# A delta rule layer whose heads draw their weight pieces from one chain, and new orders in two later layers

## The chip, the cores and the metric

The kernel runs on one core of a Trainium2 chip. The metric is the device time of one execution, in microseconds (us); lower is better.

## The reference, cut to what is computed

Two blocks of layers run over one sequence of 512 tokens, with a model width of 1024, all in fp32. The first block has a pooling mixer, a gated delta rule (the layer that most of the change is in), latent attention and again pooling. The second block has an even layer (Mamba, with a gated feed-forward in front and a causal depthwise convolution over its streams) and an odd layer (differential attention with rotary embedding). The delta rule has 8 heads; q and k have 128 rows, v and the gate z 256, and q, k and v first pass a causal convolution of 4 taps and a SiLU. Its core per head and chunk:

```python
def chunk_gated_delta_rule(q, k, v, g, beta):
    B, S, H, dk = q.shape
    dv = v.shape[-1]
    C = GDN_CHUNK
    N = S // C
    ...
    g = jnp.cumsum(g.reshape(B, N, C, H).transpose(0, 3, 1, 2), axis=-1)
    k_beta = k * beta[..., None]
    v_beta = v * beta[..., None]
    causal = jnp.tril(jnp.ones((C, C), dtype=bool))
    strict = jnp.tril(jnp.ones((C, C), dtype=bool), -1)
    diff = g[..., :, None] - g[..., None, :]
    decay = jnp.exp(jnp.where(causal, diff, -jnp.inf))
    L = jnp.where(strict, jnp.einsum('bhnid,bhnjd->bhnij', k_beta, k) * decay, 0.0)
    A = jnp.eye(C, dtype=L.dtype) + L
    rhs = jnp.concatenate([v_beta, k_beta * jnp.exp(g)[..., None]], axis=-1)
    sol = lax.linalg.triangular_solve(A, rhs, left_side=True, lower=True)
    u_ps = sol[..., :dv]
    w_cd = sol[..., dv:]
    attn = jnp.where(causal, jnp.einsum('bhnid,bhnjd->bhnij', q, k) * decay, 0.0)
    def step(state, xs):
        q_c, k_c, u_c, w_c, g_c, a_c = xs
        v_new = u_c - jnp.einsum('bhck,bhkv->bhcv', w_c, state)
        o = (jnp.einsum('bhck,bhkv->bhcv', q_c * jnp.exp(g_c)[..., None], state)
             + jnp.einsum('bhij,bhjv->bhiv', a_c, v_new))
        g_last = g_c[..., -1]
        k_dec = k_c * jnp.exp(g_last[..., None] - g_c)[..., None]
        state = state * jnp.exp(g_last)[..., None, None] + jnp.einsum('bhck,bhcv->bhkv', k_dec, v_new)
        return state, o
    ...
    _, o = lax.scan(step, state0, xs)
    return o.transpose(1, 0, 3, 2, 4).reshape(B, S, H, dv)
```

The result of a head is normalised, multiplied by its scale and by SiLU of z, and taken through the output weights.

## The kernel before, in words

A product of the large weights is done in pieces of 128 x 128 weights against 128 x 512 activations. Because the fp32 operands are split into a high and a low part, one piece is three matmuls (lines 334, 335 and 336), each one 128x512. Weights arrive by DMA as 128 x 1024 blocks, ScalarE (ACT) rounds the high part (`whi`, line 296) and GpSimd (POOL) makes the low part (`wlo`, line 311). VectorE (DVE) "takes" a finished product tile out of PSUM. Eight pieces make one tile of a projection. Tiles go round four PSUM banks, so the first piece of tile n waits until tile n-4 is taken.

The delta rule layer (about 325 to 870 us of the span) works head by head. Its own matmuls are small and wait on DVE and ACT. `work_tensor(pe, i, more)` (line 1933) is the order on TensorE (PE) for head i, and at each of 21 named sites it calls `more(site)`, which issues some pieces of the large products to fill the time. How many is a table, `PIECES` and `PIECES_BETWEEN`, at line 2318 and on. `pieces(i)` (line 2349) yields the 56 pieces that go with head i: V1 (the second half of the head's v), K of the next head, Q, V0, the gates z0 and z1 of 8 pieces each, and then four output tiles of 2 pieces each. When `work_tensor` of a head returns, a loop issues what is left of its pieces ("rest"). Head 0 also draws the first six pieces of head 1, so heads 1 to 4 have few left.

The sites in their order within a head: `kk` (k times k), `P2`, `P4`, `P8`, `PV8` (doubling steps of the triangular inverse), `X`, `X2`, `X2V`, `join`, `joined`, then for each chunk c of four `v new c`, `o c` and `kS c`. Ahead of `kk` there are three short pieces of work: the k tokens (`k_tokens`, line 1930, transposes of k), the sum over o of the head before (line 2044) and the row of the gate G (line 1963). The G row waits for "y gated 1" of the head before, since both use one bank. ACT starts from the k tokens: squares of k (line 2049), kdec (2055), the square of q (1923), ln (2141), ln o (2143), then exp (2073 and on), and at its end the N blocks (2083), for which P2 waits.

`work_vector(dve, i, fill, y_before)` (line 2163) is the order on DVE. Each `fill(site)` there makes as many takes as the table `TAKES` says; a take of q, k or v is followed by its four convolution taps (lines 1881 and 1884), spread behind later fills. For head 0 alone the set-up of the gates stands in front (`gate_vector`): six memsets (line 1810) of 128x512 or 128x256 zeros, then the rows of G in high and low parts (lines 1812 and 1814, "rows"), for which PE waits with the k tokens of head 0.

In the even layer `glu_vector` (line 1042) makes the convolution taps (line 1032) that follow the first product; `other_taps(dve, g, a)` (line 1197, work on line 1202) makes three taps of another stream. In the odd layer `rotary_tables` (line 2440) makes the cosine and sine tables of head pair 0; `cos`, `sin` (lines 3152 and 3159 to 3167) apply them, `square` (line 3124), `ln_k` (line 3130) and the exp of `lam` (line 3091) are ACT's, and the scores (line 3303) wait for kn (line 3172).

## Time and profile before

| | us |
|---|---|
| median of 3 runs | 2474.79 |
| lowest and highest | 2472.77, 2477.22 |
| the profiled execution, own time | 2474.79 |
| its span | 2473.0 |
| PE busy | 2435.5 (98%) |
| DVE busy | 1649.3 (67%) |
| POOL busy | 1191.4 (48%) |
| ACT busy | 1034.5 (42%) |
| PE clock over the span | 0.997 of full |

The profiled execution is the median run itself, so a change to its span can be set against the median directly; 1.8 us lie outside the span. Busy time of PE is modelled, with each matmul shown from its start to an end that overlaps the next. How long a matmul really holds the engine is the distance from its start to the next one's. DVE is busy in two thirds of the span, and in stretches where it is late, PE waits; an idle time of an engine other than PE costs nothing unless PE waits for it.

### The profile page before, as it was taken

The page shows a single profiled execution, that of the slowest core. Times are in us where ns is not written, and L with a number is a line of the kernel's source. Part 1 is how long each engine was busy: PE and PEld are TensorE (multiplying, and loading weights), DVE is VectorE, ACT ScalarE, POOL GpSimd, SP SyncE. Part 2 cuts the span into 40 slices and gives each one's busy share as a digit, 9 for nine tenths or more (in the row PEclk, how much of TensorE's full clock was granted, in tenths as well). Part 3 has the DMA queues.
Part 4 walks back from the last instruction along what each step waited for, and adds up shares of the span by engine and source line. Part 5 has one row for each costly group of instructions (what it writes and reads, how often), then busy time and mean ns, then how long its engine had stood idle before and what let it go on. Part 6 is the DMA issues. An engine that isn't in the chain of part 4 may idle for free.

```text
span 2473.0 us, 31476 instructions
## 1 busy us (share of the span) xinstructions
PE 2435.5 (98%) x11606; PEld 1950.2 (79%) x11606; DVE 1649.3 (67%) x2898; ACT 1034.5 (42%) x1697; POOL 1191.4 (48%) x1447
## 2 busy tenths in 40 slices
PE   9999999999999999999999999999999999999999
PEld 7888877788888787777777788888888777867777
DVE  7644687777777665434343656546998998477776
ACT  4222254444444354333333332224544668454443
POOL 7665643333343375334443366666554534644342
PEclk9999999999999999999999999999999999999999
DMA  4233221121111132222222132233322211321211
GB/s 161 86 103 111 94 82 53 59 63 66 60 61 51 53 129 86 67 79 73 80 77 79 60 103 94 87 104 101 102 94 85 72 53 52 122 77 60 69 60 43
DMA packets 60008, 198.43 MB, mean 80 GB/s; under 512 B 7248, under 2 KB 9936, under 8 KB 59856
## 3 DMA queue, kind: packets, MB, share of 16 engines
q1 hardware_dynamic: 56976, 192.90, 23.8%
q10 hardware_dynamic: 2880, 3.51, 0.6%
q8 instruction: 94, 1.54, 0.3%
q14 instruction: 58, 0.48, 0.1%
HBM read 191.93 MB, written 2.10 MB: 78 GB/s over the span
## 4 chain that ended last, share of the span: by engine, by line
PE 86%; DVE 10%; ACT 2%; issue 1%; DMA 0%; SPq 0%; ACTq 0%; DVEq 0%
PE psum L334 23%; PE psum L336 23%; PE psum L335 22%; PE psum L1939 3%; PE psum L2842 1%; PE psum L2827 1%; DVE psum L1032 1%; PE psum L2845 1%; PE psum L3303 1%; DVE e_c L1032 1%; DVE e_stg L1202 1%; PE psum L3280 1%; PE psum L2818 1%; DVE g_left L2156 1%; PE psum L2027 1%
## 5 line engine op out<-in xcount | busy, mean ns | idle before, releaser
L311 POOL TENSOR_TENSOR wlo<-raw,whi 128x256 fp32r<-128x256 f32 x1436 | 1190.9, 862 | 1255.2 <-ACT whi L296 1255.1
L334 PE MATMUL psum<-xh,whi 128*128 128x512 f32 x1800 | 732.9, 407 | 1.4 <-DVE e_stg L1202 1.4
L336 PE MATMUL psum<-xh,wlo 128*128 128x512 f32 x1800 | 705.0, 392 | 0.0
L335 PE MATMUL psum<-xl,whi 128*128 128x512 f32 x1800 | 703.7, 391 | 0.0
L296 ACT ACTIVATE whi<-raw 128x1024 fp32r<-128x1024 f32 (+1 forms) x369 | 378.4, 1031 | 723.3 <-PE psum L336 698.5
L336 PEld LDWEIGHTS psum<-xh,wlo 128*128 128x128 f32 x1800 | 339.1, 188 | 73.7
L334 PEld LDWEIGHTS psum<-xh,whi 128*128 128x128 f32 x1800 | 340.0, 189 | 72.2 <-issue 6.7
L335 PEld LDWEIGHTS psum<-xl,whi 128*128 128x128 f32 x1800 | 339.8, 189 | 67.3 <-issue 2.9
L606 DVE TENSOR_TENSOR xT<-psum,xT 128x512 f32<-128x512 f32 x232 | 155.4, 686 | 161.7 <-PE psum L336 153.7
L702 DVE TENSOR_TENSOR pool_u<-psum,R 128x512 f32<-128x512 f32 x32 | 21.9, 691 | 122.8 <-PE psum L336 122.7
L334 PE MATMUL psum<-pool_y,whi 128*128 128x512 f32 x256 | 99.6, 389 | 0.0
L335 PE MATMUL psum<-pool_y,whi 128*128 128x512 f32 x256 | 99.6, 389 | 0.0
L336 PE MATMUL psum<-pool_y,wlo 128*128 128x512 f32 x256 | 99.6, 389 | 0.0
L1032 DVE SCALAR_TENSOR_TENSOR psum<-e_ue,par,psum 128x512 f32<-128x512 f32 x112 | 79.7, 747 | 3.4 <-ACT psum L1013 3.4
L2782 DVE TENSOR_TENSOR mwork<-psum,R 128x512 f32<-128x512 f32 x16 | 11.1, 691 | 86.0 <-PE psum L336 86.0
L2871 ACT ACTIVATE mwork<-psum,nmx 128x128 f32<-128x128 f32 (+3 forms) x64 | 33.7, 528 | 82.3 <-DVE nmx L2935 82.2
L2933 DVE TENSOR_REDUCE mxs<-psum 128x1 f32<-128x128 f32 (+3 forms) x64 | 31.1, 487 | 51.6 <-PE psum L2847 51.6
L1884 DVE SCALAR_TENSOR_TENSOR g_qv<-pre,par,g_qv 128x512 f32<-128x512 f32 x72 | 62.0, 861 | 1.1
L1939 PEld LDWEIGHTS psum<-g_PU,g_left 128*128 128x128 f32 x384 | 48.4, 193 | 14.6 <-DVE g_PU L2161 6.0
L334 PE MATMUL psum<-gy,whi 128*128 128x512 f32 x128 | 56.2, 439 | 2.3 <-issue 1.2
L334 PE MATMUL psum<-cq,whi 128*128 128x512 f32 x144 | 58.1, 404 | 0.0
L1939 PE MATMUL psum<-g_PU,g_left 128*128 128x64 f32 (+1 forms) x384 | 52.1, 279 | 4.4 <-DVE g_PU L2161 2.2
(563 smaller groups left out, 4345.6 us busy)
## 6 DMA issues: line engine op xcount, KB each, us to landing
raw<-weights_dram SPq DMA_DIRECT2D x329, 512.0 KB, 3.6
raw<-weights_dram SPq DMA_DIRECT2D x40, 384.0 KB, 3.0
xin<-x_dram SPq DMA_DIRECT2D x4, 512.0 KB, 6.2
mla_xrot<-sq ACTq DMA_DIRECT2D x32, 64.0 KB, 2.0
out_dram<-xT SPq DMA_DIRECT2D x8, 256.0 KB, 2.1
par<-params_dram SPq DMA_DIRECT2D x1, 323.5 KB, 8.3
g_masks<-gdn_masks_dram ACTq DMA_DIRECT2D x1, 288.0 KB, 2.8
mwork<-positions_dram ACTq DMA_DIRECT2D x1, 256.0 KB, 3.6
```

The costliest lines, as they stand in the source:

```text
L296: act.activation(whi[:, q, 0:nk * nm * P], raw[:, q, 0:nk * nm * P], ACT.Copy).then_inc(hi_ready[q], 1)
L311: last = pool.tensor_tensor(wlo[:, q, part], raw[:, q, part], whi[:, q, part].bitcast(F32), ALU.subtract)
L334: pe.matmul(gbank(b), whi[:, q, c:c + P], h, start=k == 0, stop=False)
L335: pe.matmul(gbank(b), whi[:, q, c:c + P], l, start=False, stop=False)
L336: done = pe.matmul(gbank(b), wlo[:, q, c:c + P], h, start=False, stop=k == nk - 1)
L606: dve.tensor_tensor(xT[:, t, :], tile(sec, j, m), xT[:, t, :], ALU.add).then_inc(*taken(sec, j, m))
L1032: dve.scalar_tensor_tensor(out=out, in0=src[:, k:k + SEQ], scalar=dw[:, 32 * c + k:32 * c + k + 1], in1=old, op0=ALU.mult, op1=ALU.add).th ...
L1202: op = dve.scalar_tensor_tensor(out=stg[:, g % 2, x, s:], in0=bank(j)[:, 0:SEQ - s], scalar=conv[:, 20 * g + 5 * x + k:20 * g + 5 * x + k ...
L1884: dve.scalar_tensor_tensor(out=dst, in0=pre[:, x, k:k + SEQ], scalar=w, in1=dst, op0=ALU.mult, op1=ALU.add).then_inc(*ve.done(f"{i} tap {k ...
L1939: last = pe.matmul(wbank(b)[:, c * n:(c + 1) * n], left[:, c, :], right[:, c, :], start=True, stop=True)
L2871: act.activation(prob[:, hd, off_q[t]:off_q[t] + w], wbank(x % 4)[:, 0:w], ACT.Exp, scale=SCALE, bias=nmx[:, x:x + 1], accum_out=rs[:, x:x ...
L2933: dve.reduce_max(mxs[:, x:x + 1], wbank(x % 4)[:, 0:w], AX.X).then_inc(*ve.done(f"{i} max raw {x}"))
```

## The change

Parts of it, with the diff after them.

- **Head 0.** `gate_vector` zeroes U and Nt only; left0 and left1 are zeroed behind "rows" around the first tap of Q, left2 and left4 where the Q taps 1 to 3 stood in `work_vector`. Those three taps go behind the turn of P2, and the take of V0 that stood there goes on to `fill("V2")`. On PE, kk goes ahead of the wait for "rows", and kq (k times q) goes from behind P2 to behind P4 and its pieces.
- **One chain.** Heads 0 to 5 draw their pieces from one chain, with no loop for the rest behind heads 0 to 4. `PIECES` and `EARLY` change: head 0 issues 57 pieces, head 1 56, heads 2 to 4 54 each, against 54, 53 and 53 before (and 2 or 3 more in the loop for the rest behind heads 1 to 4). Behind `o 3` heads 1 to 4 have 8 pieces where they had 5, head 1 has 11 behind `kk` where it had 8. The `TAKES` of heads 1 to 4 get a table of their own: 3 behind `rhs 2`, and 3, 3, 2, 1 behind `v new 3`.
- **Even layer.** The three taps of stream 0 stand inside the last `glu_vector`, six taps before its end, and no longer behind it.
- **Odd layer.** ACT loads the sine and cosine table before it waits for its input; squares 2 and 3 go ahead of their neighbours (`ln_k`) and around the exp of `lam`; DVE waits for the cosines right behind take 2, and makes cos and sin of x = 0 before take 3.

```diff
...
                     tap(dve, a + 2, k)
-            def glu_vector(dve, t, other):
+            def glu_vector(dve, t, other, late=lambda: None):
                 a, b = 2 * t, 2 * t + 1
                 take_u(dve, a)
...
                 take_u(dve, b)
                 for k in range(15, TAPS):
+                    if k == TAPS - 6:
+                        late()
                     tap(dve, a, k)
                     if k - 15 < (EARLY if t == GROUPS - 1 else EARLY - 2):
...
                 small_work = dt_vector(dve)
                 for t in range(GROUPS):
-                    glu_vector(dve, t, (lambda: next(small_work, None)) if t >= 2 else (lambda: None))
+                    glu_vector(dve, t, (lambda: next(small_work, None)) if t >= 2 else (lambda: None),
+                               (lambda: other_taps(dve, 0, 0)) if t == GROUPS - 1 else (lambda: None))
                     if t == 1:
                         residual(dve, 0, KD)
                 for _ in small_work:
                     pass
-                for a in range(4):
+                for a in range(1, 4):
                     other_taps(dve, 0, a)
...
                 return kb[:, i % 2, :] if x == K else qv[:, max(0, x - 1), :]
+
+            def zeros(dve, *tiles):
+                for t0 in tiles:
+                    dve.memset(t0[:, :, :], 0.0).then_inc(*ve.done("zeros " + t0.name))
             def gate_vector(dve):
...
                    .then_inc(*ve.done("last-G"))
                 yield
-                for t0 in (U, Nt, left[0], left[1], left[2], left[4]):
-                    dve.memset(t0[:, :, :], 0.0).then_inc(*ve.done("zeros " + t0.name))
+                zeros(dve, U, Nt)
                 dve.wait_ge(*te.of("G rows"))
                 dve.tensor_copy(Ghl[0:8, :], wbank(0)[0:8, :]).then_inc(*ve.done("rows hi"))
...
                     last.then_inc(*te.done(f"{i} v tokens {h}"))
+                if i == 0:
+                    pe.wait_ge(*ae.of(f"0 silu {K}"))
+                    four(2, kc, kc, "kk")
                 pe.wait_ge(*(ve.of(f"{i - 1} y gated 1") if i else ve.of("rows")))
                 if i == 0:
...
                 pe.matmul(wbank(3), pick[:, i:i + 1].to_broadcast([P, P]), Ghl[:, :], start=True, stop=True)\
                   .then_inc(*te.done(f"{i} G row"))
-                four(2, kc, kc, "kk")
+                if i:
+                    four(2, kc, kc, "kk")
                 more("kk")
                 pe.wait_ge(*ve.of(f"{i} P"))
                 pe.wait_ge(*ae.of(f"{i} N blocks"))
                 four(2, left[0], Pw, "P2", 64)
-                if i == 0:
-                    more("P2")
-                pe.wait_ge(*ae.of(f"{i} silu {QQ}"))
-                pe.wait_ge(*ae.of(f"{i} exp G row"))
-                four(3, kc, qc, "kq")
+
+                def kq():
+                    pe.wait_ge(*ae.of(f"{i} silu {QQ}"))
+                    pe.wait_ge(*ae.of(f"{i} exp G row"))
+                    four(3, kc, qc, "kq")
+
                 if i:
-                    more("P2")
+                    kq()
+                more("P2")
                 pe.wait_ge(*ae.of(f"{i} k dec"))
                 pe.wait_ge(*ve.of(f"{i} P2 turned"))
                 four(0, left[1], PU, "P4")
                 more("P4")
+                if i == 0:
+                    kq()
                 if i:
                     pe.wait_ge(*ae.of(f"{i - 1} ln o"))
...
                 dve.tensor_tensor(V, Pw, over(one64), ALU.add).then_inc(*ve.done(f"{i} V1"))
                 if i == 0:
-                    for k in (1, 2, 3):
-                        tap(dve, QQ, 0, k)
+                    zeros(dve, left[2], left[4])
                 turn(dve, i, "N above", lambda to, of: N[rows(to), :, rows(of)], Nt, False, [(1, 0), (3, 2)])
                 dve.wait_ge(*ve.of(f"{i} N above turned"))
...
                 if i:
                     y_before(0)
+                else:
+                    for k in (1, 2, 3):
+                        tap(dve, QQ, 0, k)
                 fill("P2")
                 dve.wait_ge(*te.of(f"{i} P4"))
...
             SITES = ["kk", "P2", "P4", "P8", "PV8", "X", "X2", "X2V", "join", "joined", "v new 0", "o 0", "kS 1", "v new 1",
                      "o 1", "kS 2", "v new 2", "o 2", "kS 3", "v new 3", "o 3"]
-            EARLY = [8, 3, 3, 3, 3, 2, 2, 2, 3, 3]
-            PIECES = {i: EARLY + [2] * 6 + [1] * 4 + [5] for i in (1, 2, 3, 4)}
-            AHEAD = 6
-            PIECES[0] = EARLY + [2] * 6 + [1] * 4 + [AHEAD]
-            PIECES[H - 1] = EARLY + [2, 1] * 5 + [6]
+            EARLY = [8, 3, 4, 3, 3, 2, 2, 2, 2, 2]
+            PIECES = {i: EARLY + [2] * 5 + [1] * 5 + [8] for i in (2, 3, 4)}
+            PIECES[0] = [8, 4, 5, 3, 3, 2, 2, 2, 3, 3] + [2] * 6 + [1] * 4 + [6]
+            PIECES[1] = [11] + EARLY[1:] + [2] * 4 + [1] * 6 + [8]
+            PIECES[H - 1] = [8, 3, 3, 3, 3, 2, 2, 2, 3, 3] + [2, 1] * 5 + [6]
             PIECES_BETWEEN = EARLY + [2] * 10 + [6]
-
-            TAKES = {0: {"P2": 2, "V2": 2, "A": 1, "V8": 2, "X": 2, "V32": 3, "U": 1, "Y": 1, "U joined": 1,
+            CHAINED = 5
+
+            TAKES = {0: {"V2": 3, "A": 2, "V8": 2, "X": 2, "V32": 3, "U": 1, "Y": 1, "U joined": 1,
                          "v new 0": 2, "state 0": 2, "rhs 1": 2, "v new 1": 2, "state 1": 1, "rhs 2": 1, "v new 2": 1,
                          "v new 3": 1},
...
                              "v new 0": 1, "state 0": 1, "rhs 1": 1, "v new 1": 1, "state 1": 1,
                              "rhs 2": 1, "v new 2": 1, "state 2": 1, "rhs 3": 1, "v new 3": 2, "o summed": 2}}
+            TAKES.update({i: {"V2": 1, "V8": 1, "X": 1, "V32": 2, "U": 1, "Y": 1, "U joined": 1,
+                              "v new 0": 2, "state 0": 2, "rhs 1": 2, "v new 1": 2, "state 1": 2, "rhs 2": 3,
+                              "v new 2": 1, "v new 3": (3, 3, 2, 1)[i - 1], "o summed": 2} for i in (1, 2, 3, 4)})
             TAKES_BETWEEN = {"V2": 1, "V8": 1, "X": 1, "V32": 2, "U": 1, "Y": 1,
                              "U joined": 1, "v new 0": 2, "state 0": 2, "rhs 1": 2, "v new 1": 2,
...
                                 yield
-                of_head = [pieces(i) for i in range(H)]
+                chained = itertools.chain.from_iterable(pieces(i) for i in range(CHAINED + 1))
                 for i in range(H):
-                    rest = itertools.chain(of_head[0], itertools.islice(of_head[1], AHEAD)) if i == 0 else of_head[i]
+                    rest = chained if i <= CHAINED else pieces(i)
                     counts_of = dict(zip(SITES, PIECES.get(i, PIECES_BETWEEN)))
...
                             next(rest, None)
                     work_tensor(pe, i, more)
-                    for _ in rest:
-                        pass
+                    if i >= CHAINED:
+                        for _ in rest:
+                            pass
                 hi, lo, ready = ([t for h in (H - 2, H - 1) for t in (y_operand(h)[a] if a == 2 else
                                                                      [y_operand(h)[a][:, d, :] for d in range(2)])]
...
                 take_in(dve, QQ, 0)
                 next(gates)
+                zeros(dve, left[0])
                 tap(dve, QQ, 0, 0)
+                zeros(dve, left[1])
                 dve.wait_ge(masks_in, 16)
                 for i in range(H):
...
                 dve.tensor_scalar(lam[:, 6:7], lam[:, 5:6], -LAM0, None, ALU.add).then_inc(*vbs.done("-lam"))
                 dve.wait_ge(*vbs.at("-lam"))
-                dve.wait_ge(*ab.at("cos"))
             def tables_scalar(act):
+                act.preload_act_table_set("trig_and_small")
                 rotary_tables(None, act, vbs, ab, "scalar", pos_i, cosT[:, :], sinT[:, :], tmp, None, "scalar")
+
+            def lam_scalar(act):
                 act.wait_ge(*tb.at("lam"))
                 act.activation(lam[:, 2:4], wbank(3)[:, 0:2], ACT.Exp).then_inc(*ab.done("exp"))
...
                 hi_after(act, S, 0, 2, True)
                 tables_scalar(act)
-                ln_k(act, 0, 0)
+                square(act, 0, 2)
+                lam_scalar(act)
+                square(act, 0, 3)
                 hi_after(act, S, 0, 3, True)
-                square(act, 0, 2)
-                square(act, 0, 3)
-                ln_k(act, 0, 1)
+                for x in range(2):
+                    ln_k(act, 0, x)
                 ln_q(act, 0)
                 exp_kq(act, 0)
...
                 tables_vector(dve)
                 take(dve, 2, xq[:, 2, :])
+                dve.wait_ge(*ab.at("cos"))
+                cos(dve, 0, 0)
+                sin(dve, 0, 0)
                 take(dve, 3, xq[:, 3, :])
                 lam_vector(dve)
-                cos(dve, 0, 0)
-                cos(dve, 0, 1)
-                sin(dve, 0, 0)
-                for x in range(2, 4):
+                for x in range(1, 4):
                     cos(dve, 0, x)
                 for x in range(1, 4):
...
```

Three places in the order of the instructions. The names of rows: `g_left0` to `g_left4` and `g_Nt`, `g_PU`, `U` are operands of the triangular inverse, `Ghl` are the G rows, `g_qv` is a stream of q or v in its taps, `pre` a projection just taken.

**DVE, head 0, from the zeros of the gates to Q's first tap.** Before:

```order
MEMSET g_Nt 128x256
MEMSET g_left0 128x512
MEMSET g_left1 128x512
MEMSET g_left2 128x512
MEMSET g_left4 128x512
CAST Ghl<-psum 8x512
TENSOR_TENSOR Ghl<-psum,Ghl 8x512
COPY gcol<-g_ts 128x32
TENSOR_SCALAR g_qv<-pre,par 128x512
```

And now:

```order
MEMSET g_Nt 128x256
CAST Ghl<-psum 8x512
TENSOR_TENSOR Ghl<-psum,Ghl 8x512
COPY gcol<-g_ts 128x32
MEMSET g_left0 128x512
TENSOR_SCALAR g_qv<-pre,par 128x512
MEMSET g_left1 128x512
```

Four memsets have left the stretch ahead of the G rows. Two of them stand behind it, and two further on in the head.

**PE, from the end of head 2 to the first pieces of head 3** (k tokens at line 1930, o sum at 2044, G row at 1963, kk at 1939 in the numbering of before). Before, where the loop for the rest issues three pieces behind the o sum, of which one is shown:

```order
L336 MATMUL psum<-gy,wlo 128x512
L1930 MATMUL psum<-cst,g_k 128x128 x4
L2044 MATMUL psum<-kkc,cst 128x512
L334 MATMUL psum<-gy,whi 128x512
L335 MATMUL psum<-gy,whi 128x512
L336 MATMUL psum<-gy,wlo 128x512
...
L1963 MATMUL psum<-Ghl,g_pick 128x512
L1939 MATMUL psum<-g_k 128x128 x4
L334 MATMUL psum<-xh,whi 128x512
```

And now:

```order
L336 MATMUL psum<-xh,wlo 128x512
L1936 MATMUL psum<-cst,g_k 128x128 x4
L2058 MATMUL psum<-kkc,cst 128x512
L1972 MATMUL psum<-Ghl,g_pick 128x512
L1945 MATMUL psum<-g_k 128x128 x4
L334 MATMUL psum<-xh,whi 128x512
```

The three pieces between o sum and G row are gone; they stand ahead of the k tokens.

**DVE, head 2, behind rhs 2** (which is line 2267 before and 2283 now; the copy is v new 2, and `gs` the take of z). Before:

```order
L2267 SCALAR_TENSOR_TENSOR vb<-psum,g_small,vb 128x256
L1884 SCALAR_TENSOR_TENSOR g_qv<-pre,par,g_qv 128x512 x2
L2271 COPY d<-psum 128x256
L1874 TENSOR_TENSOR gs<-psum,R 128x512
L2279 SCALAR_TENSOR_TENSOR d<-d,egl,psum 128x256
```

And now:

```order
L2283 SCALAR_TENSOR_TENSOR vb<-psum,g_small,vb 128x256
L1890 SCALAR_TENSOR_TENSOR g_qv<-pre,par,g_qv 128x512 x2
L1880 TENSOR_TENSOR gs<-psum,R 128x512
L2287 COPY d<-psum 128x256
L1880 TENSOR_TENSOR gs<-psum,R 128x512
```

A take of z has moved in between the two taps and the copy.

## Rows read from the trace of the kernel before

**Rows 1.** The page: PE's busy time, share of the span and number of matmuls.
```profile
PE 2435.5 (98%) x11606; PEld 1950.2 (79%) x11606; DVE 1649.3 (67%) x2898; ACT 1034.5 (42%) x1697; POOL 1191.4 (48%) x1447
```

**Rows 2.** Waits of PE, whole span: us in total, times, longest us.
```profile
PE psum L3303 <- DVE o_kn L3172: 2.0, 1, 2.0
...
PE psum L3116 <- ACT o_rr L3124: 1.7, 4, 0.6
...
PE psum L1963 <- DVE vb L2293: 1.6, 2, 1.4
...
PE psum L334 <- DVE e_stg L1202: 1.4, 1, 1.4
...
PE psum L2044 <- DVE kkc L2289: 0.9, 2, 0.6
...
PE psum L1939 <- DVE g_small L2221: 0.7, 4, 0.2
```

**Rows 3.** Windows: length; PE, PEld, DVE, ACT, POOL busy; PEclk, DMA share, GB/s.
```profile
359.60:363.00 3.40, 3.40 (x13) 2.92 (x13) 1.89 (x6) 1.91 (x4) 3.40 (x6) 0.50 0.00 0
...
472.20:475.60 3.40, 3.40 (x13) 3.01 (x14) 3.26 (x8) 3.36 (x5) 0.00 (x0) 0.50 0.00 0
...
419.10:422.50 3.40, 3.40 (x23) 3.10 (x24) 3.21 (x10) 1.79 (x4) 2.36 (x4) 1.00 0.00 0
...
2192.50:2195.90 3.40, 3.40 (x10) 2.37 (x8) 1.47 (x7) 1.00 (x4) 1.06 (x2) 0.50 0.40 110
```

**Rows 4.** Timeline of PE in head 0: start, us, line, tiles, [idle before <- releaser].
```profile
345.63 0.66 PE L1930 MATMUL psum<-cst,g_k 128*128 128x128 f32 x4 [1.18 <-DVE Ghl L1814]
...
358.32 1.16 PE L1939 MATMUL psum<-g_qv,g_k 128*128 128x128 f32 x8 [2.46 <-ACT g_qv L1913]
```

**Rows 5.** Timeline of DVE in head 0: the zeros, and Q's taps 1 to 3.
```profile
342.22 2.11 DVE L1810 MEMSET g_left<- 128x512 f32 x4
...
352.81 2.32 DVE L1884 SCALAR_TENSOR_TENSOR g_qv<-pre,par,g_qv 128x512 f32<-128x512 f32 x3
```

**Rows 6.** Timeline of PE in head 1: k tokens, and P2.
```profile
408.75 0.60 PE L1930 MATMUL psum<-cst,g_k 128*128 128x128 f32 x4
...
419.03 1.08 PE L1939 MATMUL psum<-g_PU,g_left 128*128 128x64 f32 x8 [1.47 <-ACT g_left L2083]
```

**Rows 7.** Timeline of PE, head 2 to 3: v new 2, k tokens, o sum, G row, first piece.
```profile
521.00 0.59 PE L2027 MATMUL psum<-vb,U 128*128 128x256 f32 x2
...
530.47 0.60 PE L1930 MATMUL psum<-cst,g_k 128*128 128x128 f32 x4
531.07 1.12 PE L2044 MATMUL psum<-kkc,cst 128*128 128x512 f32 x2
...
534.10 0.39 PE L1963 MATMUL psum<-Ghl,g_pick 128*128 128x512 f32 x1
...
535.13 0.48 PE L334 MATMUL psum<-xh,whi 128*128 128x512 f32 x1
```

**Rows 8.** Timeline of ACT, head 2 to 3: two table loads and the N blocks.
```profile
533.82 1.28 ACT L2141 ACT_TABLE_LOAD   x1
535.11 0.30 ACT L2141 ACTIVATE g_small<-g_small,bias 128x4 f32<-128x4 f32 x1
...
536.00 1.28 ACT L2073 ACT_TABLE_LOAD   x1
...
539.36 1.25 ACT L2083 ACTIVATE g_left<-N 32x128 f32<-32x128 f32 x4
```

**Rows 9.** Timeline of DVE, head 2: two taps, the copy v new 2, a take.
```profile
519.78 1.89 DVE L1884 SCALAR_TENSOR_TENSOR g_qv<-pre,par,g_qv 128x512 f32<-128x512 f32 x2
521.64 0.42 DVE L2271 COPY d<-psum 128x256 f32<-128x256 f32 x1
521.98 0.68 DVE L1874 TENSOR_TENSOR gs<-psum,R 128x512 f32<-128x512 f32 x1
```

**Rows 10.** Timeline of ACT, odd layer: the load of the table of sine.
```profile
2170.77 1.28 ACT L2461 ACT_TABLE_LOAD   x1
```

## The prediction, made before the changed kernel had run

> **What bounds the kernel now.** I read the page first: PE is busy in 98% of the span [rows 1], so nothing is won by making another engine shorter, and only two kinds of time can move. One is PE's idle time, the other is time in which PE runs at half its clock. The number of matmuls stays, so pieces that move from one site to another cost nothing by themselves. The list of PE's waits comes second [rows 2]: the largest single ones are 2 us and less, against a span of 2473 us. The windows with the clock come third [rows 3]: after some idle times PE shows a granted clock of 0.50 (1.2 GHz) for 3.4 us, in which it does the work of 1.7 us. So a fall costs 1.7 us on top of the wait. The profiled run is the median run (2474.8), and the sum is made against it. A measurement of this kernel can tell about 0.2%, here 5 us, from no change.
>
> **Head 0.** PE waits 1.2 us for the G rows with its k tokens, and 2.5 us for SiLU of Q with kq [rows 4]; the second idle is followed by the stretch of half clock at 359.6 [rows 3]. A restart costs about 0.15 us more than the idle shown, so I count 1.3 and 2.6. The four memsets that leave the path to the G rows take 2.1 us [rows 5], more than the first wait, so that one goes. kq now comes behind P4 and its five pieces, and SiLU of Q has ended by then (its taps take 2.3 us [rows 5] and move some 2 us behind where they were, but kq moves further). So the second wait goes, and its fall of the clock. What is late next: the P chain of DVE. P is needed by PE about 0.6 us before DVE has it, since PE now arrives 1.3 us sooner at P2 and DVE only 0.5; P2's turn is again about 0.6 late; and the taps now lie in front of the turns behind P4, so a third wait of 0.6 appears near V8 and X. Minus 1.3, 2.6 and 1.7, plus 1.8: **-3.8 us**. Bounds: -5.6 (no new wait) to -1.5 (new waits of twice the size).
>
> **Head 1.** P2 comes 10.3 us behind the k tokens and waits for ACT's N blocks for 1.5 us of it [rows 6]. Three more pieces behind kk (9 matmuls at 0.23 us each, 2.05 us) fill that, and P8's short wait (one of four of 0.2 us, 0.3 with the restart [rows 2]) goes too: -1.8. Then the cost of starting early: head 1 is now nine pieces ahead of its own takes. An output tile needs its bank, and the bank is free only when DVE has taken V0 or z0. V0's take lies behind v new 1, z0's is the third take behind rhs 2 and so behind two taps (1.9 us [rows 9]). By a replay of the two engines' orders I get stalls of 1.4 us (V0), 3.0 (z0), 1.3 (first take of v new 3) and 2.2 at P2 of the next head (below), together +7.9. The waits for the sum of o and for "y gated" there go (0.6 and 1.4 us [rows 2]), and the half clock behind them at 472.2 [rows 3]: -3.7. Head 1 gives +7.9 - 3.7 - 1.8 = **+2.4 us**.
>
> **Heads 2 to 4.** Two new stalls in each. *At v new 2*: before, PE has two pieces in kS 2, starts v new 2 at 521.00 [rows 7], and one piece later the state's matmuls, whose operand is the copy; DVE makes it (0.42 us) right behind two taps, at 521.64 [rows 9], in time. Now kS 2 has one piece (0.68 us less), and a take (0.68 us [rows 9]) lies between the taps and the copy. PE is ready 0.7 sooner and the operand comes 0.7 later: a stall of **1.4 us**. *At P2*: ACT's chain from the k tokens to the N blocks has no gap in it. It starts when the k tokens are done at 530.5 [rows 7], holds two table loads of 1.28 us [rows 8], and ends with the N blocks at 540.6 [rows 8], 10.1 us later, and P2 can start 0.15 behind. Before, PE filled this with 0.6 (k tokens), 0.9 (o sum), three pieces 2.05, G row and kk 1.03, and eight pieces of 5.5: 10.1, just enough. Now the three pieces stand ahead of the k tokens and PE arrives at P2 after 8.0 us: a stall of **2.2 us**, for the next head, of which a part may show at the G row instead. Credits: P8's wait (0.3) and two restarts (0.2). So 3.6 - 0.5 = 3.1 us a head, **+9.3 us** for three. Bounds: 0 (ACT or DVE turn out to be ahead by as much) and +12. Heads 5 to 7 lose waits of 0.3 us at P8 and PV8 three times: **-1.0**.
>
> A rule of the Trainium skill can be weighed here. ACT's next function starts 0.01 us behind the end of its table load (535.10 and 535.11 [rows 8]), so a switch costs 1.3 us here, and the sum goes by that. The Trainium skill ("ScalarE: Activation LUTs", What ACT_TABLE_LOAD costs) says that a drain of about 1.38 us comes on top of the load, 2.66 us a switch. By it ACT's chain would be 2.8 us longer, each stall at P2 5.0 us, and the sum 11.2 us higher. The trace does not agree.
>
> **Even layer.** PE waits 1.4 us once for the first of the stream's taps [rows 2]. They move to about 6 taps before DVE's last stretch ends and are ready before PE arrives; the last convolution taps become 2.3 us later, for which nobody waits at once. **-1.5 us**, bounds -1.6 and -0.5.
>
> **Odd layer.** The load of the sine table (1.28 us) starts only when its input is there [rows 10]; preloaded, the cosines come 1.3 us sooner. DVE used to make take 3 and lam first and then all of cos and sin; now it uses its idle time for x = 0. That brings kn about 2.7 us forward, against PE's wait of 2.0 [rows 2], which goes with its half clock at 2192.5 [rows 3], and squares 2 and 3 go ahead, which saves a wait of 0.6 [rows 2]. But PE arrives 0.6 sooner, and kn is in time by only 0.1. -2.0 - 0.6 - 1.7 = **-4.3 us**, bounds -4.6 and -2.7 (kn late by some tenths, with a fall of the clock).
>
> **The sum.** -3.8 + 2.4 + 9.3 - 1.0 - 1.5 - 4.3 = +1.1 us, 2475.9, if the clock stays up. It will not: idle times of 2 to 2.5 us were followed by a fall three times (head 0, head 1's end and the odd layer [rows 3]), while one of 1.5 us in head 1 was not (419.1 [rows 3]). The new stalls are one of 3.0 us in head 1 and four of 2.2 us at P2. I count three falls, 5.1 us: **2481.0 us**. With all five it is 2484.4.
>
> **The rivals.**
>
> *The clock holds.* PE is fully busy up to each of the new stalls, as it was before the 1.5 us one. Then the sum without falls is 2475.9: within 0.2%. Against it: before the falls in head 0 and the odd layer PE was busy too, and those idles were 2.5 and 2.0 us, the size of P2's new one.
>
> *The takes are not late, and it gets faster.* The mechanism is DVE's lead behind rhs 2. The two taps there take 0.95 us each [rows 9] and Q's three in head 0 only 0.77 each [rows 5], so their length depends on what runs beside them; and a stall of PE at P2 gives DVE, which idles little there, time to catch up for the rest of the head. If the takes come in time by that, head 1's bank stalls (5.7) and the three at v new 2 (4.2) do not exist, and neither does the fall in head 1 (1.7). From 2481.0 that leaves 2469.4: faster by 0.2%. It decides at the copy: DVE must reach it 1.4 us sooner than in my replay. For it speaks the spread of the taps, which is worth 0.4 us of it; against it that DVE waits for PE's kS products before rhs 2, so that a lead won earlier is lost there.
>
> *The odd layer's gain does not come, or the clock falls at each stall.* kn is in time by 0.1 us only, by my count. If it is late PE still waits 0.5 and the clock falls, 2.2 us more; with falls at all four P2 stalls (3.4) the time is 2486.6.
>
> *The chain does nothing.* If the stall at P2 is filled since PE is behind ACT for another reason (say it starts late on weights), the four P2 stalls (8.8) and two of their falls (3.4) go: 2468.8. The rows speak against it: PE waits nowhere for weights in the list [rows 2].
>
> **How the numbers follow.** My forecast, 2481.0 with three falls and its neighbours of two or more: 0.45. The clock holds or falls once or twice: 0.25. The takes are in time: 0.14. P2's stall is filled: 0.06. Clock falls at each, or the odd layer without gain: 0.10. The bounds of head 0 (2 us up or down) and of the odd layer (1.6 up) smear each. The two rivals on the faster side hold 0.20, of which some ends within 0.2%, and some of the second's does not; I put 0.18 on faster. Within 0.2% (2469.8 to 2479.7): 0.30. Slower: 0.52. The range that holds 8 in 10 goes from 2469.5, where "the takes are in time" lies, to 2486.0. The likeliest case alone has 2478 to 2485.
>
> **What would show it.** Right: new idle times of PE at P2 of heads 2 to 5, ended by the N blocks of ACT (or by "y gated" at the G row in front of it), about 2.2 us between them; PE waiting for the copy in v new 2 in heads 2 to 4; head 1's product of an output tile waiting for a take; the idles at 358.3, 419.0, 1889.3 and 2191.0 gone; three stretches of clock 0.50 gone and about three new ones within 450 to 700 us. Wrong: no row with the N blocks among PE's waits, or idle times in head 0 over 2 us. If the four P2 stalls are there and the time is still under 2475, the step that failed is the falls of the clock.

## The result: 13.8 us slower, the ratio 1.0059

| | before, us | changed, us |
|---|---|---|
| median | 2475.15 | 2488.93 |
| lowest and highest | 2472.77, 2477.22 | 2487.51, 2491.57 |
| runs | 4 | 4 |
| the profiled execution, own time | 2474.79 | 2487.51 |
| its span | 2473.0 | 2485.6 |
| PE busy | 2435.5 | 2435.7 |

The ratio of the changed kernel to the one before is 1.0059, with a 95% interval of 1.0047 to 1.0071. It is slower, as forecast, by 13.8 us where 6.2 were forecast, and its time lies 2.9 us above the top of the range (2486.0). PE's busy time has not moved (2435.5 and 2435.7), so the 12.6 us of the span are idle time of PE: span less busy time went from 37.5 to 49.9 us. Both profiled executions have four falls of the clock in them, at other places, so time at half clock cancels in this difference. The profiled execution of the changed kernel is its fastest of four; of the 13.8 us between the medians it shows 12.7. One execution of the kernel with the even layer's taps alone took 8110 us, and its figures below are those of the other ten.

PE's waits in the changed kernel over the whole span (columns as in [rows 2]; the line numbers of what moved are 6 to 25 higher):

```profile
PE psum L1945 <- ACT g_left L2097: 9.0, 5, 2.2
PE psum L1945 <- DVE g_PU L2175: 5.0, 7, 0.8
PE psum L334 <- DVE gs L1880: 3.2, 2, 3.0
PE psum L2048 <- DVE d L2287: 3.1, 3, 1.0
PE psum L334 <- issue: 2.7, 2, 1.5
...
PE psum L334 <- DVE xT L606: 1.9, 2, 1.2
...
PE psum L2048 <- ACT vb L2318: 1.3, 1, 1.3
PE psum L1945 <- DVE g_left L2170: 1.2, 2, 0.7
PE psum L3141 <- ACT o_rr L3149: 1.1, 3, 0.4
PE psum L334 <- DVE pre L1875: 1.1, 1, 1.1
```

The waits of [rows 2] for e_stg, for kn and for "y gated" are gone from the list. In their place stand the N blocks (first row: four of 2.2 us, one each in heads 2 to 5, and one of 0.2 in head 1), the copy v new 2 (`d`, L2287: three of 1.0), and takes (`gs`, `xT`, `pre`). The second row is one that I had not foreseen: `g_PU`, 5.0 us in seven waits, where the kernel before had 2.2 in six.

**Where the time went.** Between the G rows of two heads one can take the time from the timeline, and set it off against the pieces issued there, at 0.681 us each (three matmuls of 0.227 from start to start). Positive is slower. The last column is the forecast with the falls of the clock that it takes away, and without the three new ones that it adds.

| stretch | before: G row at, pieces to the next | changed | difference less pieces | forecast without new falls |
|---|---|---|---|---|
| head 0 | 346.04, 54 | 346.22, 57 | -3.5 | -3.8 |
| head 1 | 410.68, 50 | 409.41, 56 | +1.6 | +1.9 |
| head 2 | 472.06, 56 | 476.47, 54 | +2.2 | +1.4 |
| head 3 | 534.10, 56 | 539.39, 54 | +5.4 | +3.1 |
| head 4 | 594.64, 56 | 603.98, 54 | +5.4 | +3.1 |
| head 5 | 655.16, 64 | 668.56, 61 | +6.3 | +1.6 |
| head 6 | 721.10, 64 | 738.73, 64 | +0.8 | -0.3 |
| even layer | | | -1.7 | -1.5 |
| odd layer | | | -4.4 | -4.3 |

(The numbers of the last two rows are from where the same matmul starts in both traces. At the first layer's start the two executions differ by 0.7 us, which has nothing to do with the change. Head 1 of the kernel before has 50 pieces and none left over for the loop behind it; the sections above put it at 53.)

Heads 3, 4 and 5 each hold one fall of the clock, as the windows show (length; PE, PEld, DVE, ACT, POOL busy; PEclk, DMA share, GB/s), and head 0, at the place of [rows 3], holds none:

```profile
359.60:363.00 3.40, 3.40 (x24) 3.08 (x23) 3.31 (x8) 3.36 (x6) 2.07 (x3) 1.00 0.00 0
...
485.90:489.30 3.40, 3.40 (x23) 3.13 (x24) 3.21 (x10) 2.66 (x5) 2.34 (x4) 1.00 0.00 0
...
549.30:552.70 3.40, 3.40 (x15) 3.23 (x15) 3.03 (x8) 2.17 (x4) 2.82 (x5) 0.50 0.00 0
614.10:617.50 3.40, 3.40 (x16) 3.11 (x15) 2.93 (x8) 2.26 (x5) 3.03 (x4) 0.51 0.00 0
679.00:682.40 3.40, 3.40 (x14) 3.01 (x13) 2.65 (x7) 2.25 (x4) 3.35 (x5) 0.50 0.02 5
```

The window at 485.9 is behind P2 of head 2, with the same stall of 2.2 us in front, and the clock stays up there. Three falls were forecast, for the stall in head 1 and the four at P2 together; three came, all at P2, in heads 3, 4 and 5. In the kernels below that keep all of these stalls the same stretch has four, three and two, so that the count came out right is in part luck.

PE's timeline from the k tokens of head 3 to its P2 shows the main term (pieces left out; compare [rows 7]):

```profile
538.50 0.60 PE L1936 MATMUL psum<-cst,g_k 128*128 128x128 f32 x4
538.93 1.02 PE L2058 MATMUL psum<-kkc,cst 128*128 128x512 f32 x2
539.39 0.79 PE L1972 MATMUL psum<-Ghl,g_pick 128*128 128x512 f32 x1
540.02 1.05 PE L1945 MATMUL psum<-g_k 128*128 128x128 f32 x8
...
548.78 0.63 PE L1945 MATMUL psum<-g_PU,g_left 128*128 128x64 f32 x4 [2.21 <-ACT g_left L2097]
```

From 538.50 to 548.78 are 10.28 us, to the hundredth what P2 took behind the k tokens in head 1 of the kernel before [rows 6]. The G row follows the o sum at once, with no wait for "y gated" in front of it.

### The profile page after: what moved, and what is told of

Read it like the earlier page. It is cut to its first block, busy times and chain, and to the rows that moved or that the text cites. A ratio compares the mean times of both kernels' runs of the same rounds, so it can differ in the third digit from the quotient of the medians.

```text
span 2485.6 us, 31475 instructions
## 1 busy us (share of the span) xinstructions
PE 2435.7 (98%) x11606; PEld 1952.5 (79%) x11606; DVE 1643.5 (66%) x2898; ACT 1033.7 (42%) x1697; POOL 1188.0 (48%) x1447
## 4 chain that ended last, share of the span: by engine, by line
PE 86%; DVE 8%; ACT 3%; issue 1%; DMA 0%; SPq 0%; ACTq 0%; DVEq 0%
PE psum L334 23%; PE psum L336 23%; PE psum L335 23%; PE psum L1945 2%; PE psum L2865 1%; PE psum L2850 1%; PE psum L2868 1%; DVE g_qv L1890 1%; PE psum L3328 1%; DVE e_c L1032 1%; PE psum L3305 1%; DVE e_stg L1204 1%; PE psum L2841 1%; PE psum L2051 1%; PE psum L2041 1%
## 5 line engine op out<-in xcount | busy, mean ns | idle before, releaser
L702 DVE TENSOR_TENSOR pool_u<-psum,R 128x512 f32<-128x512 f32 x32 | 21.9, 691 | 122.8 <-PE psum L336 122.7
L1890 DVE SCALAR_TENSOR_TENSOR g_qv<-pre,par,g_qv 128x512 f32<-128x512 f32 x72 | 63.5, 882 | 1.2
```

Source lines behind the costliest of these rows:

```text
L1890: dve.scalar_tensor_tensor(out=dst, in0=pre[:, x, k:k + SEQ], scalar=w, in1=dst, op0=ALU.mult, op1=ALU.add).then_inc(*ve.done(f"{i} tap {k ...
```

## The experiments

Two theories stood against each other. **A:** the loss is a number of separate stalls of PE, each made by one thing that now stands too far back on ACT or DVE, and they add up; the other edits (head 0, even, odd) gain by themselves. **B:** being ahead on the chain costs as such, and a stall that is taken away comes back at the next site, or in a fall of the clock. All kernels were compared with the kernel before on their own chip, where its median was 2475.04, 2474.73 or 2474.24 us. Waits below are those of the one profiled execution. A wait costs some 0.15 us more than the idle time shown, by an estimate from the rows: the matmul ahead of it is shown for 0.39 us, where the next would have started after 0.227. This is the "restart" below.

### Everything but the chain

```diff
-                chained = itertools.chain.from_iterable(...)
+                of_head = [pieces(i) for i in range(H)]
+                rest = itertools.chain(of_head[0], itertools.islice(of_head[1], AHEAD)) if i == 0 else of_head[i]
...
-            PIECES[0] = [8, 4, 5, 3, 3, 2, 2, 2, 3, 3] + [2] * 6 + [1] * 4 + [6]
+            PIECES[0] = [8, 4, 5, 3, 3, 2, 2, 2, 3, 3] + [2] * 6 + [1] * 4 + [3]
```

The other rows of `PIECES` and the `TAKES` of heads 1 to 4 are those of before.

> The tables of pieces and takes and the loop for the rest are those of the kernel before; the new orders of head 0, of the even and of the odd layer stay. Theory A (the loss is made by the chain alone, in stalls of heads 1 to 6; head 0, even and odd layer gain 3.5, 1.7 and 4.4 us by the trace of the change): 2465.5 us, 9.6 under the kernel before, and PE's waits for the N blocks in heads 2 to 5 gone. Theory B (the changed kernel's gains in head 0 and the odd layer come only from a clock that happened not to fall, as the loss does from one that fell): 2471 to 2475, with stretches of half clock in head 0 or the odd layer.

Measured: 2467.16 us (before on the same chip 2475.04), ratio 0.9968, interval 0.9955 to 0.998. Its waits for the N blocks are down to one, of head 1:

```profile
PE psum L1972 <- DVE vb L2309: 1.6, 2, 1.4
...
PE psum L1945 <- ACT g_left L2097: 1.1, 1, 1.1
```

Theory A's number was 2465.5, the other's 2471 to 2475. The whole of the loss is the chain's: with it 2488.9, without it 2467.2. The other edits together are worth 7.9 us; the interval (4.9 to 11.1 us) holds the 9.6 that I summed from the one trace, and leaves out theory B's. Half clock in the odd layer is still there, at 2240 and 2373 us (before at 2192 and 2380), and the fall behind head 1's last wait, at 472 in the kernel before, did not come in this execution, though the wait is the same (1.4 us). So a part of the 7.9 can be falls that happened not to come.

### Three pieces behind the o sum

```diff
                 pe.matmul(wbank(1), ones, osq[0], start=True, stop=True).then_inc(*te.done(f"{i} o sum"))
+                more("o sum")
...
-            PIECES = {i: EARLY + [2] * 5 + [1] * 5 + [8] for i in (2, 3, 4)}
+            PIECES = {i: EARLY + [2] * 5 + [1] * 5 + [5, 3] for i in (2, 3, 4)}
```

Head 1's 8 behind `o 3` become 5 and 3 likewise; the other heads get a 0 for the new site.

> The changed kernel, with three of the eight pieces behind o 3 moved behind the o sum in heads 1 to 4. Theory A (the k tokens come too late against PE's work up to P2): the four stalls of 2.2 us at P2 go with their restarts, 9.3 us, and the three falls of the clock that follow them, 4.9 us: about 2474.5 us. Theory B (being ahead on the chain is what costs, wherever the pieces stand): a stall at P2 goes, but takes its place at the banks or at X2V: 2480 to 2486.

Measured: 2475.96 us, ratio to before 1.0005, interval 0.9996 to 1.0014. Theory A had 2474.5, theory B 2480 to 2486. So this single edit gives back 13 us of the 13.8, though not a piece has left the chain. PE in head 3 of this kernel (pieces left out):

```profile
535.81 0.60 PE L1936 MATMUL psum<-cst,g_k 128*128 128x128 f32 x4
536.24 1.02 PE L2058 MATMUL psum<-kkc,cst 128*128 128x512 f32 x2
539.16 0.39 PE L1972 MATMUL psum<-Ghl,g_pick 128*128 128x512 f32 x1
...
546.10 1.07 PE L1945 MATMUL psum<-g_PU,g_left 128*128 128x64 f32 x8 [0.19 <-ACT g_left L2098]
```

P2 starts 10.29 us behind the k tokens again, but PE idles for 0.19 us of it, not 2.21. The other waits of the changed kernel are all there in this one (`g_PU` 5.1, `gs` 3.2, `d` 3.2 us in its list), so no wait has moved to another site. The row of the N blocks went from 9.0 to 0.9 us, and the profiled execution has two falls fewer, two and not four (the three at P2 are gone, and one came behind the 3.0 us stall in head 1): 8.1 and 3.4 us, of the 11.6 by which its span is shorter.

### z0's take behind v new 2

```diff
-                              "v new 0": 2, "state 0": 2, "rhs 1": 2, "v new 1": 2, "state 1": 2, "rhs 2": 3,
-                              "v new 2": 1, ...
+                              "v new 0": 2, "state 0": 2, "rhs 1": 2, "v new 1": 2, "state 1": 2, "rhs 2": 3 if i == 1 else 2,
+                              "v new 2": 1 if i == 1 else 2, ...
```

> The changed kernel, with the take of z0 behind v new 2 and not behind rhs 2 in heads 2 to 4. Theory A (the take holds up the copy v new 2): the three idles of 1.03 us for the copy shrink to 0.3 or less, 2.1 to 3.1 us won, 2486 to 2487. Theory B (the copy is late since the two taps in front of it are slow): the idles stay over 0.7 us, the time within 1 us of 2488.9. A third outcome: the take that is now later holds up the bank of an output tile, an idle at line 334 in its place.

Measured: 2485.81 us, against 2488.93 of the changed kernel (ratio to before 1.0043, interval 1.003 to 1.0055). Its row for the copy:

```profile
PE psum L2048 <- DVE d L2287: 1.4, 3, 0.5
```

3.1 us became 1.4, so the take is the larger part of that stall, though theory A had 0.3 us or less for what is left in each head. That 0.5 us has two candidates that were not told apart: one piece fewer in front of it (0.68 us), and the two taps ahead of the copy, 1.97 us in head 2 of this kernel where two without POOL beside them take 1.5. The profiled spans differ by 1.7 us, as the waits do, and the medians by 3.1; the executions of the changed kernel alone spread over 4 us. Head 1 keeps the old order. By the order of the code the output tile's piece in its `kS 2` needs the bank that this take frees, and v new 2 stands behind that piece; this was not tried.

### The rounding of a block, later

```diff
-                hi_after(act, S, 0, hi[2], True)
+                if not 1 <= i <= 5:
+                    hi_after(act, S, 0, hi[2], True)
                 silu(act, V1, i)
+                if 1 <= i <= 5:
+                    hi_after(act, S, 0, hi[2], True)
```

What called for this run are the timelines of ACT, DVE and POOL in the changed kernel, head 3, ahead of X2V:

```profile
565.00 0.60 ACT L2127 ACTIVATE g_left<-psum 128x512 f32<-128x512 f32 x1 [5.20 <-PE psum L1945]
565.49 1.05 ACT L296 ACTIVATE whi<-raw 128x1024 fp32r<-128x1024 f32 x1
```
```profile
566.18 1.82 DVE L2331 TENSOR_TENSOR gy<-vb,gy 128x512 fp32r<-128x512 f32 x2
567.93 1.22 DVE L1890 SCALAR_TENSOR_TENSOR g_qv<-pre,par,g_qv 128x512 f32<-128x512 f32 x1
569.18 0.64 DVE L2170 STREAM_TRANSPOSE g_left<-psum 32x128 f32<-32x128 f32 x2
569.85 0.42 DVE L2175 TENSOR_TENSOR g_PU<-g_PU,psum 128x256 f32<-128x256 f32 x1
```
```profile
566.62 3.81 POOL L311 TENSOR_TENSOR wlo<-raw,whi 128x256 fp32r<-128x256 f32 x4 [3.93 <-ACT whi L296]
```

The same instructions of head 3 in the kernel before:

```profile
556.36 1.28 DVE L2315 TENSOR_TENSOR gy<-vb,gy 128x512 fp32r<-128x512 f32 x2
557.56 0.74 DVE L1884 SCALAR_TENSOR_TENSOR g_qv<-pre,par,g_qv 128x512 f32<-128x512 f32 x1
558.35 0.64 DVE L2156 STREAM_TRANSPOSE g_left<-psum 32x128 f32<-32x128 f32 x2
```

There POOL idled, since PE had not yet freed the slot of the block. In the chained kernel PE frees it earlier, ACT rounds the block at its first turn, and POOL works out the low part beside DVE. The DVE instructions with two operands in SBUF take 0.5 us more each; the transpose and the copy out of PSUM don't change. DVE is then a microsecond late with `g_PU`, for which X2V waits.

> The changed kernel, with ACT rounding the third block of weights of heads 1 to 5 behind SiLU of V1 and not in front of it. The trace of the change shows X2V waiting 0.8 us for DVE in heads 2 to 5, where two DVE instructions of two operands took 1.23 and 1.22 us beside POOL's low parts, and 0.68 and 0.74 in head 6, without POOL. Theory A (POOL's work, started sooner by the earlier rounding, slows DVE on the path to X2V): those instructions fall to 0.7, and the wait of 0.8 (0.95 with the restart) goes in four heads, some 3.5 us in all, 2485.5. Theory B (X2V is late for what PE does before it, not for POOL): the wait stays at 0.5 or more, and the time within 1 us of 2488.9.

Measured: 2482.83 us (ratio to before 1.0029, interval 1.0017 to 1.0042), 6.1 us under the changed kernel. DVE in head 3 of this kernel:

```profile
563.58 1.28 DVE L2334 TENSOR_TENSOR gy<-vb,gy 128x512 fp32r<-128x512 f32 x2
564.78 0.75 DVE L1890 SCALAR_TENSOR_TENSOR g_qv<-pre,par,g_qv 128x512 f32<-128x512 f32 x1
```

And its row of the list:

```profile
PE psum L1945 <- DVE g_PU L2178: 1.1, 2, 0.8
```

The five waits of heads 1 to 5 are gone (head 1's was in the kernel before too), and only head 0's are left. Five of 0.95 us, with the restart, are 4.8 us. The other 1.3 us is less than the executions of either kernel spread (3 to 4 us), and is not explained: the profiled execution has one fall fewer in these heads and one more in the odd layer. Theory A's number was 2485.5, for four heads and not five. This settles the mechanism: nothing was changed but the place of five roundings, and the instructions that were long are short again. The rest of the changed kernel's layer says the same. Of its later taps of q, k and v (L1890) 53 ran with no low part beside them and took 0.75 us in the median, and 32 ran beside one nearly all the time and took 1.10; of the single products of L2331 six took 0.68 and five 1.23. The Trainium skill ("GPSIMD Engine Reference", Key points) says that GpSimd shares its SBUF interfaces with VectorE, and that DVE instructions in a two-port mode or with two SBUF inputs contend with it. These rows agree, with 0.74 against 1.22 us for an instruction on two operands (L1890 in head 3); the page gives no size for it.

### Heads 5 and 6

```diff
-                hi_after(act, S, 0, hi[3], True)
+                if i != 6:
+                    hi_after(act, S, 0, hi[3], True)
                 v_beta(act, i, 1)
+                if i == 6:
+                    hi_after(act, S, 0, hi[3], True)
...
+            TAKES[5] = dict(TAKES_BETWEEN, **{"v new 3": 2})
```

In head 6 of the changed kernel ACT rounds a block that PE has just released, and v beta queues behind it:

```profile
774.29 1.06 ACT L296 ACTIVATE whi<-raw 128x1024 fp32r<-128x1024 f32 x1 [5.03 <-PE psum L336]
775.26 0.82 ACT L2318 ACTIVATE vb<-psum,g_small 128x256 f32<-128x256 f32 x2
```
```profile
776.13 0.70 PE L2048 MATMUL psum<-d,kdec 128*128 128x256 f32 x2 [1.26 <-ACT vb L2318]
```

In head 5 a piece behind `o 3` starts after an idle time of 1.50 us that the list puts down to "issue". DVE's take of an output tile, which frees a bank, ends its first half as that piece starts:

```profile
731.86 0.47 PE L334 MATMUL psum<-gy,whi 128*128 128x512 f32 x1 [1.50 <-issue]
```
```profile
731.07 1.28 DVE L606 TENSOR_TENSOR xT<-psum,xT 128x512 f32<-128x512 f32 x2
```

> The changed kernel, with ACT's second v beta of head 6 in front of the rounding of the fourth block (it stood behind), and one more take behind v new 3 in head 5. Theory A (both waits, of 1.26 us for v beta in head 6 and 1.50 us ahead of a piece behind o 3 in head 5, come from work standing one place too far back on ACT and DVE): both go, 2.8 us in all, 2486.1. Theory B (they come from PE's arrival alone): the waits move to the next site, and the time stays within 1 us of 2488.9.

Measured: 2487.49 us (2483.69 to 2488.03), ratio to before 1.0047, interval 1.0033 to 1.0061. Both waits are gone from its trace, and no other came; its idle time of PE is 3.0 us less. The median moved by 1.4 us only. The profiled run of this kernel, 2485.7 us in span, has six falls of the clock, against four in that of the changed kernel (three above and one at 2392.5). Two of the three that the changed kernel's profile does not have:

```profile
461.50:464.90 3.40, 3.01 (x7) 2.45 (x8) 0.81 (x3) 1.57 (x2) 1.38 (x3) 0.50 0.30 122
488.80:492.20 3.40, 3.40 (x12) 2.72 (x11) 2.08 (x5) 2.23 (x5) 3.40 (x5) 0.50 0.00 0
```

Both stand behind stalls that the two kernels share, the 3.0 us in head 1 and P2 of head 2. So which stalls are followed by a fall differs between kernels, or executions, with equal stalls. By the waits theory A is right, by the median time the run is inconclusive. The clock granted in each execution helps here: at 0.997 the changed kernel took 2487.5 and 2488.0 us and this one 2483.7, at 0.996 2489.9 against 2487.5 to 2488.0, at 0.995 2491.6 against 2487.5. At an equal clock it is 2 to 4 us faster, in line with the 2.8 of the waits. With four and five executions that is a hint and no proof.

### All the repairs together

All four edits above, in the changed kernel.

> The changed kernel with all edits at once: three pieces behind the o sum, z0's take behind v new 2 in heads 2 to 4, the later rounding of heads 1 to 5, v beta and the take of heads 6 and 5. Theory A (the losses are separate and add up): 13.0, 3.1, 6.1 and 2.8 us under 2488.9, 2464 us, with the bank waits of head 1 (1.1, 3.0 and 1.2 us) left. Theory B (they are one loss seen at several places): 2470 to 2474, as o_sum3 alone nearly has.

Measured: 2467.01 us, ratio to before 0.9971, interval 0.996 to 0.9981. As a time that decides nothing: it lies 3 us above theory A's number (2464) and 3 us below theory B's (2470 to 2474), and is 21.9 us of the 25.0 that the four gave or promised singly. The waits decide it. Singly the four took 8.1 us (N blocks), 1.7 (the copy), 3.9 (`g_PU`) and 2.8 us (heads 5 and 6) from PE's list, 16.5 together; all at once they took 16.9 (8.1, 1.8, 4.2 and 2.8). So the stalls are separate and add up, as theory A says. What did not add up is the rest of the single gains, 13.0 us for 8.1 of waits, 3.1 for 1.7 and 6.1 for 3.9, in which there are falls of the clock and the spread of the medians. What PE still waits for in heads 1 to 7:

```profile
PE psum L334 <- DVE gs L1880: 3.2, 2, 3.0
...
PE psum L334 <- DVE xT L606: 1.9, 2, 1.2
...
PE psum L2048 <- DVE d L2294: 1.3, 3, 0.4
...
PE psum L334 <- DVE pre L1875: 1.1, 1, 1.1
...
PE psum L1945 <- ACT g_left L2098: 0.9, 5, 0.2
```

The chain with its stalls repaired is as fast as the kernel with no chain at all (2467.2). What it has left are mainly head 1's waits for banks (3.0, 1.2 and 1.1 us); the second wait in each of the rows `gs` and `xT` is head 7's and was there before.

### The best version

The kernel without the chain, and in it the later rounding for head 1 alone, and for head 7:

```diff
-                             "U joined": 1,
+                             "U joined": 2,
```

> The kernel without the chain (2467.2 us), with the later rounding in head 1 alone and one more take behind U joined in head 7. Theory A (POOL beside DVE makes the wait of 0.8 us at X2V in head 1; the take of an output tile makes those of 1.2 and 0.7 us in head 7): 2464.5 us. Theory B (head 1's wait is POOL's but the takes of head 7 are bound by PE's own products): 2466.2, and head 7 unchanged.

Measured: 2462.28 us (2461.05 to 2462.64), ratio 0.9949 to before, interval 0.9936 to 0.9961. It beats both kernels, by 12.4 and 26.6 us. X2V's wait in head 1 and both waits of head 7 (1.2 and 0.7 us) are gone from its trace. The forecast of theory A was 2464.5. 4.9 us against the kernel without the chain are more than the 3.0 of the waits; the two profiled executions have the same number of falls, and where the rest comes from was not found.

### The other edits alone

The odd layer's order alone, in the kernel before:

> The kernel before with the odd layer's new order alone. Theory A (both waits there, 0.6 and 2.0 us, and the half clock behind them go): 2470.8 us, 4.3 under before. Theory B (the clock is as likely to fall elsewhere as it was there, so that only the waits count): 2472.4.

Measured: 2472.16 us against 2474.73, ratio 0.9987, interval 0.9978 to 0.9995. Both waits are gone, and kn is in time:

```profile
2188.58 0.49 PE L3305 MATMUL psum<-o_kn,o_qr 64*128 64x128 f32 x4
```

The gain is 2.6 us, next to theory B's number, but the interval (1.2 to 5.4 us) holds theory A's 4.3 as well. The clock no longer falls at 2192. In this kernel's profile it falls at 2380, as before, and at two places of the layer where it did not fall before:

```profile
2243.20:2246.60 3.40, 3.40 (x11) 2.72 (x11) 3.14 (x6) 2.93 (x7) 1.98 (x2) 0.50 0.12 41
2311.50:2314.90 3.40, 3.40 (x10) 2.61 (x9) 2.77 (x5) 2.62 (x5) 1.17 (x2) 0.50 0.32 112
2379.80:2383.20 3.40, 3.40 (x10) 2.63 (x9) 2.07 (x3) 1.81 (x5) 0.36 (x1) 0.50 0.47 152
```

That profile is of its slowest execution (2474.09 us), so it shows that falls can come elsewhere, and not that they do so in the median.

The taps of the even layer alone:

> The kernel before with the even layer's moved taps alone. Theory A (the one wait of 1.4 us for the first stream goes with its restart): 1.6 to 1.7 us under before, 2473.3. Theory B (the convolution taps that are now 2.3 us later are waited for): no gain, and an idle ahead of the next stream in its place.

Measured: 2472.26 us against 2474.24, ratio 0.9991, interval 0.9982 to 1.0. The wait of 1.4 us is gone and none came for it, which is theory A. The gain of 2.0 us agrees with its 1.6 to 1.7, but the interval holds no gain as well.

Head 0's new order alone, with 3 pieces behind `o 3`:

> The kernel before with head 0's new order alone (its zeros, its taps of Q, kk and kq), 54 pieces in it as before. Theory A (two waits of 1.2 and 2.5 us and the half clock behind the second go, four new waits of 0.5 to 0.8 us come): 3.5 us under before, 2471.5. Theory B (the fall of the clock only moves to the next idle): 2473.2.

Measured: 2472.35 us against 2474.24, ratio 0.9993, interval 0.9984 to 1.0002. The two waits and the half clock at 359.6 are gone from its trace, and the waits that the changed kernel has in head 0 stand there too (0.5, 0.5, 0.8 and 0.7 us). The gain of 1.9 us lies at theory B's 1.8 and not at theory A's 3.5, but the interval (4.0 us down to a loss of 0.5) holds both.

The three gains, 2.6, 2.0 and 1.9 us, sum to 6.4; the three edits together gave 7.9. With intervals of 2 us to either side of each that is no contradiction, and it shows the limit: an edit of under 2 us is better read from its wait than from its time.

## Why the prediction was right and wrong

**What was right.** The direction; that the loss is the chain's; and each stall that the sum names. P2 in heads 2 to 5: 2.2 us forecast, 2.21 measured in each. The takes in head 1: 1.4, 3.0 and 1.3 forecast, 1.07, 3.04 and 1.21 measured. v new 2 in heads 2 to 4: 1.4 forecast, 1.03 measured, 1.2 with the restart. Head 0: -3.8 against -3.5, with waits of 0.5, 0.5, 0.8 and 0.7 us in it. Even layer -1.5 against -1.7, odd layer -4.3 against -4.4 in the profiled runs. Three falls of the clock were counted, and three came in the delta rule layer, in part by luck, as said above. One reading was wrong and did no harm: 530.5 is the start of the k tokens and not their end (ACT starts behind them, at 531.10). The sum counts PE's 8.0 us from that same start, and the measured 10.28 less 2.21 is 8.07.

**The step that failed** is the one on heads 2 to 7: "Credits: P8's wait (0.3) and two restarts (0.2)" and "Heads 5 to 7 lose waits of 0.3 us at P8 and PV8 three times: -1.0". It took the work around the moved pieces to be as long and as early as before, and so counted only waits that go. (Those of heads 5 and 6 went; head 7 kept its 0.18 us and got 0.24 more.) Three kinds of wait came that have no term in the sum:

- X2V in heads 2 to 5 waits 0.8 us for DVE (0.95 with the restart), 3.8 us in all. The rounding comes sooner, and POOL's low parts with it, beside two DVE instructions on the way to X2V. The later rounding took these waits away.
- A piece of an output tile in head 5 waits 1.5 us for a bank, since the chain brings head 5 three pieces ahead of its takes. One more take ahead of it took the wait away.
- v beta 1 in head 6 comes 1.3 us late, since a rounding that PE releases just then stands in front of it on ACT. The other order took this wait away.

Those are 3.8, 1.6 and 1.4 us with the restart, 6.8 in all, less the 0.6 by which v new 2 came smaller: 6.2. The table of heads leaves 6.1 to find between its last two columns, with the three falls taken off (1.7 each). The median lies 7.9 us above the forecast; of the rest 0.7 is the start of the first layer, and 1.4 is what the profiled execution lies below the median, against 0.3 that the even and odd layer came better.

The rival "the takes are not late" argued from just this contention, with the sign turned round: that taps of 0.95 us [rows 9] might run faster in the new order. Ahead of the copy in head 2 the two took 1.88 us, as before (1.89), so the takes were late; on the way to X2V other instructions ran slower. The two other things that were left out, the bank in head 5 and the order on ACT in head 6, are of the same kind as head 1's stalls, which a replay of the engines' orders had found; it was not taken on to heads 5 and 6.

**The range** reached up to the rival with more falls of the clock. It had no case for more stalls of the kind that was forecast, though the chain shifts every block of heads 1 to 6 against three other engines.

**The gains of the odd layer and head 0** are right as waits. Their medians alone, 2.6 and 1.9 us, are smaller than the 4.3 and 3.5 that count a fall of the clock with them; the intervals hold both, so whether a fall that goes in one place comes in another in the mean of many executions is not shown.

## What to carry to other kernels

Where pieces are moved from behind an event to in front of it, compare the time from that event to its consumer with the work that is left between them: here 10.3 us of ACT's chain against 8.0 us of PE's work, and three pieces put back gave 13 us, 8.1 of it waits. Here being ahead with filler work also freed slots earlier, and so started the preparation of the next blocks earlier, on POOL beside DVE (3.8 us of waits for X2V) and on ACT in front of v beta (1.3 us); follow those queues too. Count a wait at its own size, and a fall of the clock behind it as a chance only.

## What the runs showed of the hardware

DVE instructions with two operands in SBUF took 1.22 us beside POOL's TENSOR_TENSOR and 0.74 without it (L1890), and 1.82 against 1.28 for two of L2331, of which mostly the second ran beside POOL; POOL's own four took 3.81 us, where eight in that stretch have a median of 0.74 each; both engines' instructions get longer. DVE's transpose (0.64 us for two) and its sum with an operand in PSUM (0.42 us) took the same with and without POOL. One thing more stands in the same trace: the first tap of a stream, which reads one tile of SBUF (L1887), took 0.47 to 0.49 us alone, and three of the four that ran wholly beside a low part took 0.91 to 1.00.

Stalls of PE of equal length and place are followed by 3.4 us at half clock in some kernels and not in others. The stall of 3.0 us in head 1 was followed by it in the profiled executions of all five other kernels that have the chain, and not in that of the changed one. Of the kernels that keep the 2.2 us stalls at P2, the changed one has it behind those of heads 3, 4 and 5, that with the take moved behind heads 3 and 5, that with the later rounding behind head 4, and that with the repairs of heads 5 and 6 behind heads 2, 4 and 5. The runs do not show what decides it.
